# A diffusion trunk on one core: moving modulation tiles out of the front units, and handing every second low half to GpSimd

## The reference, cut to what matters

```python
sh1, sc1, g1, sh2, sc2, g2 = split(silu(c) @ w_mod + b_mod)     # modulation, one set for each group of tokens
h  = rmsnorm(x, norm1_g) * (1 + sc1) + sh1
u, q, k, v, z, xbc, dt = split(h @ w_in)                        # pooling, attention, state-space scan
gates = sigmoid(h @ w_gate + b_gate)
merged = sum(gate_i * (branch_i @ w_branch_i))                  # three branches
x  = x + g1 * (merged @ w_out)
h2 = rmsnorm(x, norm2_g) * (1 + sc2) + sh2
a, b = split(dwconv3(h2 @ w_up))
x  = x + g2 * ((silu(a) * b) @ w_down)
```

## Time and profile before

| what | us |
|---|---|
| three runs | 1495.09, 1491.16, 1492.04 (median 1492.04) |
| span of the profiled execution, first to last instruction | 1489.1 |
| PE busy | 1371.9 |
| DVE busy | 1080.2 |
| ACT busy | 650.6 |
| POOL busy | 221.1 |
| mean granted TensorE clock | 0.965 of full speed |

### The profile page before, as it was taken

One profiled execution on the slowest core, in us unless ns is written; L12 is line 12 of the kernel. 1 busy time (PEld: TensorE's weight loads), 2 busy tenths in 40 slices (PEclk: granted clock), 3 DMA queues, 4 the chain that ended last, 5 costly groups with the idle time before them and its releaser, 6 DMA issues.

```text
span 1489.1 us, 20142 instructions
## 1 busy us (share of the span) xinstructions
PE 1371.9 (92%) x7704; PEld 1320.6 (89%) x7704; DVE 1080.2 (73%) x1827; ACT 650.6 (44%) x1025; POOL 221.1 (15%) x202
## 2 busy tenths in 40 slices
...
GB/s 366 112 145 222 230 110 87 111 87 85 99 114 113 133 148 145 156 133 246 244 128 113 205 220 155 87 112 85 85 94 106 140 95 160 156 155 126 128 129 43
DMA packets 58143, 208.93 MB, mean 140 GB/s; under 512 B 6720, under 2 KB 8768, under 8 KB 56640
## 3 DMA queue, kind: packets, MB, share of 16 engines
...
...
HBM read 203.95 MB, written 3.68 MB: 139 GB/s over the span
## 4 chain that ended last, share of the span: by engine, by line
PE 73%; DVE 15%; ACT 6%; issue 4%; POOL 1%; DMA 1%; SPq 0%; ACTq 0%; DVEq 0%
PE acc L718 21%; PE acc L720 21%; PE acc L719 21%; DVE junk_front L1373 6%; DVE wl L1322 3%; PE mix L948 2%; PE mix L926 2%; PE mix L705 1%; ACT cv L1059 1%; PE mix L853 1%; DVE gates L1482 1%; ACT wh L1025 1%; POOL wl L598 1%; PE mix L881 1%; DMA head<-in_whead_dram 1%
## 5 line engine op out<-in xcount | busy, mean ns | idle before, releaser
L718 PE MATMUL acc<-hh,wh 128*128 128x386 f32 x1600 | 569.7, 356 | 56.0 <-POOL wl L598 25.3
L720 PE MATMUL acc<-hh,wl 128*128 128x386 f32 x1600 | 555.0, 347 | 0.0
L719 PE MATMUL acc<-hl,wh 128*128 128x386 f32 x1600 | 554.5, 347 | 0.0
L1322 DVE TENSOR_TENSOR wl<-raw,wh 128x1024 fp32r<-128x1024 f32 (+1 forms) x264 | 325.8, 1235 | 164.9 <-ACT wh L1025 162.6
L718 PEld LDWEIGHTS acc<-hh,wh 128*128 128x128 f32 x1600 | 311.5, 195 | 70.7 <-POOL wl L598 29.8
L1025 ACT ACTIVATE wh<-raw 128x1024 fp32r<-128x1024 f32 (+1 forms) x280 | 291.2, 1041 | 166.7 <-PE acc L720 166.7
L719 PEld LDWEIGHTS acc<-hl,wh 128*128 128x128 f32 x1600 | 313.2, 196 | 2.9 <-issue 0.6
L720 PEld LDWEIGHTS acc<-hh,wl 128*128 128x128 f32 x1600 | 311.4, 195 | 0.0
L1373 DVE SCALAR_TENSOR_TENSOR junk_front<-rawm,crow 128x1024 f32<-128x1024 f32 x96 | 155.3, 1654 | 0.0
L718 PE MATMUL acc<-ah,wh 128*128 128x386 f32 x352 | 119.4, 339 | 0.0
L719 PE MATMUL acc<-al,wh 128*128 128x386 f32 x352 | 119.3, 339 | 0.0
...
## 6 DMA issues: line engine op xcount, KB each, us to landing
...
```

The costliest lines, as they stand in the source:

```text
L718: mm(out, sh, mhi, start=start, stop=False)
L719: mm(out, sh, mlo, start=False, stop=False)
L720: return mm(out, sl, mhi, start=False, stop=stop)
L1322: tt(wl[:, s, 0:n], raw[:, raw_slot(u), 0:n], wh[:, s, 0:n].bitcast(F32), ALU.subtract).then_inc(lo_done, 1)
```

## The change

Three things change.

1. `mod_after` becomes a table, `MOD_PLACES`. In layer 0 the front carries 16 tiles behind units 8 to 23 and none behind 0 to 7; 8 tiles stand behind units 62 to 69 (the last branches and OUT), 14 behind every third UP unit and 22 behind DOWN units 116 to 137. So layer 0 also makes the first 28 tiles of layer 1, which then has 12 behind units 12 to 23 and 8 in UP. For units 62 to 69 there is a further copy of the silu rows, `crow_late`: a load on POOL at unit 58, and two tanh and two silu instructions at unit 61.
2. `POOL_LO` grows from 8 to 63 units a layer: 3 to 14, then the odd ones from 27 to 65 and from 75 to 135.
3. POOL's program becomes one loop over the units, in which the low half of unit u+3 comes first and the other work has its place by unit (pooling at 12, 14, 17, 20; merges two at a time at 57 to 60).

```diff
-POOL_LO = range(AHEAD, AHEAD + 8)
+POOL_LO = frozenset([*range(AHEAD, AHEAD + 12), *range(MIX0 + 3, OUT0 + 3, 2), *range(UP0 + 3, NU - 4, 2)])
+FRONT = range(UU0, MIX0)
+LATE_ROWS = BRANCH0 + 9
+LATE = range(LATE_ROWS + 1, LATE_ROWS + 9)
+LATE_DONE = OUT0 + 6
...
+def mod_places():
+    tiles = [(l, m) for l in range(DEPTH) for m in range(MODT)][MOD_HEAD:]
+    units = [(0, u) for u in FRONT] + [(0, u) for u in LATE]
+    units += [(0, UP0 + 3 * i + 2) for i in range(14)] + [(0, DOWN0 + i) for i in range(22)]
+    units += [(1, MIX0 - 12 + i) for i in range(12)] + [(1, UP0 + 5 * i + 4) for i in range(MODT - MOD_G2)]
+    return dict(zip(units, tiles, strict=True))
...
 def mod_after(l, u):
-    if u < MOD_G2 - MOD_HEAD:
-        return (l, MOD_HEAD + u)
-    if UP0 <= u < DOWN0 and (u - UP0) % G2_EVERY == G2_EVERY - 1 and (u - UP0) // G2_EVERY < MODT - MOD_G2:
-        return (l, MOD_G2 + (u - UP0) // G2_EVERY)
-    m = u - DOWN0 - 2
-    return (l + 1, m) if 0 <= m < MOD_HEAD and l + 1 < DEPTH else None
+    return MOD_PLACES.get((l, u))
...
+POOLING = (UU0 + 4, UU0 + 6, UU0 + 9, UU0 + 12)
...
+                for u in range(NU):
+                    if u == UP0:
+                        group_done(pool, l, G_OF[(OUT, KT - 1)])
+                        pool.dma_start(crow[:, :, :], cvec_rows).then_inc(crow_in, 16)
+                    if u + AHEAD in POOL_LO:
+                        lo(l, u + AHEAD)
+                    if u == 4:
+                        clear_pads(l)
+                    if u in POOLING:
+                        pooling(l, POOLING.index(u))
...
+                    if BRANCH0 + 5 <= u < BRANCH0 + 9:
+                        for j in (2 * (u - BRANCH0 - 5), 2 * (u - BRANCH0 - 5) + 1):
+                            pool.wait_ge(gb_done, count(l, 24, KT + j))
+                            nc.gpsimd.tensor_tensor(gates[:, j, :], gates[:, j, :], gates[:, KT + j, :], ALU.add) \
+                                .then_inc(mg_done, 1)
+                    if (l, u) == (0, LATE_ROWS - 3):
+                        pool.wait_ge(h_lo, count(l, NSPLIT, SP_Z + 3))
+                        pool.dma_start(crow_late[:, :, :], cvec_rows).then_inc(crow_in, 16)
+                    if OUT0 <= u < UP0:
+                        sum_square(u - OUT0, KT * (2 * l + 1))
...
+                    if (l, u) == (0, LATE_ROWS):
+                        row_tanh(1, crow_late, junk_late)
...
-                junk = junk_front if u < UP0 else junk_ffn
+                junk, rows = (junk_front, crow) if u < MIX0 else (junk_late, crow_late) if u < UP0 else (junk_ffn, crow)
...
+                    if (l, u) == (0, LATE_ROWS):
+                        rows_silu(1, crow_late, junk_late)
                     modulation(l, u)
-                    if u == MOD_G2 - MOD_HEAD - 1:
-                        summed(l, MOD_HEAD, MOD_G2)
+                    if u == MIX0 - 1:
+                        summed(l, MOD_HEAD, MOD_HEAD + KT)
+                        step.then(ts(g1h[:, :, :], mod[:, 2 * KT:3 * KT, :], 0.5, None, ALU.mult))
+                    if u == LATE_DONE:
+                        summed(l, MOD_HEAD + KT, MOD_G2)
                         scale_of(sc2, prm_("n2g", 0, KT), 4 * KT).then_inc(scale_ready, 1)
```

More of the change, by code:

```diff
@@ L84 @@
 DOWN0 = U_OF[(DOWN, 0, 0)]
-G2_EVERY = 5
-G2_LAST = UP0 + G2_EVERY * (MODT - MOD_G2) - 1
-HEAD_LAST = DOWN0 + MOD_HEAD + 1
-PREP = HEAD_LAST + 1
-POOL_LO = range(AHEAD, AHEAD + 8)
-MIX0 = U_OF[(ZZ, 0, 0)]
+PREP = DOWN0 + MOD_HEAD + 2
+MIX0 = U_OF[(ZZ, 0, 0)]
+UU0, BRANCH0, OUT0 = U_OF[(UU, 0, 0)], U_OF[(BRANCH, 0, 0)], U_OF[(OUT, 0, 0)]
+POOL_LO = frozenset([*range(AHEAD, AHEAD + 12), *range(MIX0 + 3, OUT0 + 3, 2), *range(UP0 + 3, NU - 4, 2)])
+LO_NUMBER = {}
+_n = [0, 0]
+for _u in range(DEPTH * NU):
+    _n[_u % NU in POOL_LO] += 1
+    LO_NUMBER[_u] = _u % NU in POOL_LO, _n[_u % NU in POOL_LO]
+FRONT = range(UU0, MIX0)
+LATE_ROWS = BRANCH0 + 9
+LATE = range(LATE_ROWS + 1, LATE_ROWS + 9)
+LATE_DONE = OUT0 + 6
 def closing_unit(g):
@@ L99, in lo_number @@
 def lo_number(n):
-    on_pool = n % NU in POOL_LO
-    return on_pool, sum((i % NU in POOL_LO) == on_pool for i in range(n + 1))
+    return LO_NUMBER[n]
 def done_after(u):
@@ L287, in build @@
             junk_front = sb("junk_front", [P, 2, D], where=a)
+        with ExitStack() as a:
+            sb("under_late", [P, 24 * T + 8 * T], where=a)
+            crow_late = sb("crow_late", [P, 2, D], where=a)
+            junk_late = sb("junk_late", [P, 2, D], where=a)
         with ExitStack() as a:
@@ L663, in _ @@
[L663 to L677 removed]
+                pool.wait_ge(pads, l + 1)
@@ new lines, in pooling @@
+                pool.wait_ge(u_in, count(l, 4, j))
+                step.then(nc.gpsimd.tensor_tensor(tmp[0][:, 1:UW], ut[:, j, 0:UW - 1], ut[:, j, 1:UW], ALU.add))
+                lo, cur = 1, 0
+                for i in range(j):
+                    s = 1 << i
+                    lo += s
+                    hi = UW - (lo - 1)
+                    step.then(nc.gpsimd.tensor_tensor(tmp[1 - cur][:, lo:hi], tmp[cur][:, lo - s:hi - s],
+                                                      tmp[cur][:, lo + s:hi + s], ALU.add))
+                    cur = 1 - cur
```

158 lines of the change are left out of this document (72 added, 86 removed).

## The result

The change takes **1531.8 us** (median of 4 runs, 1531.1 to 1534.7) against 1492.8 for the kernel before (1491.2 to 1495.1): ratio 1.0266, 95% interval 1.0251 to 1.0280. It is slower by 39 us. The profiled execution has a span of 1532.9; it was the slowest of its four, and that of the kernel before the fastest of its own, so differences of the two profiles come out some 5 us larger than the 39.0 of the medians. Beside the other runs the kernel before took 1492.6 to 1493.9 (median of each set), and their ratios are against that.

A forecast was written before the change was run, and what follows sets the result against it. PE was taken as the bound in UP and DOWN, DVE with POOL's blocks in the fronts. Terms -44.2 + 12.8 + 12.6 + 2.7 + 37.5 + 9.1 = +30.5 on 1492.0 gave 1522.5 us; eight-in-ten range 1464 to 1542.

The forecast's parts named there:

- main case: Whole kernel: low halves on POOL block DVE and the change is slower, 1500 to 1542 us, chance 0.68.
- central step: Wherever DVE has no time to spare: each low half moved to POOL costs DVE 2.13 us and saves 1.13.
- fronts, units 4 to 23, both layers: Without tiles beside the early units, PE runs at its own pace: gains of 25.6 and 24.0 us.
- late hand-over to the attention: Later pooling brings DVE to the attention about 5.1 us late, 2.3 to spare: 2.7 us given back per layer.
- attention slots: In the attention, POOL's low half falls on ACT's exponentials and costs nothing.
- scan: POOL's low half holds DVE, costing 1.6 us in each of four steps, two layers: +12.8 (0 to 19).
- branches and OUT, layer 0: Low halves on POOL, late silu rows and tiles load a full DVE: +12.6 us (7 to 16).
- UP and DOWN, layer 0: Tiles and blocks make DVE the bound, last update at 798.4 against 760.2: +37.5 us (0 to 48).
- UP, layer 1: Blocks and eight tiles make DVE late, PE ending at 1389.6 against 1380.46: +9.1 us (0 to 14).
- blocks that nobody feels: Rival, chance 0.20: DVE's waits absorb the blocks; UP, scan and most of DOWN cost nothing: -31, 1461 us.
- Blocks only beside tiles: Rival, chance 0.07: UP's products escape, DOWN pays blocks and six more tiles, scan half: -5, 1487 us.
- the fronts do not run free: Rival, chance 0.05: POOL's one queue or ACT holds front units near 6.9 us, removing the gain: about 1560 us.

The follow-up runs named there:

- front_only: The change, but POOL makes low halves only for units 3 to 14, all others back on DVE: 1463.3 us.
- nmb_cols: The whole change, but the attention's two-column nmb multiplication is two instructions of one column each: 1523.4 us.
- ffn_only: The change, but POOL makes low halves only for units 3 to 14 and every second one of UP and DOWN: 1502.3 us.
- after_dve: The change without any low half on POOL, pooling at units 9 to 12 instead of 12 to 20: 1460.6 us.

## Why the prediction was right, and where it was off

The direction, the mechanism and the range held: 1531.8 for a predicted 1522.5, in the range of 1500 to 1542 of the main case. Its central step, that a low half on POOL blocks DVE for longer than the 1.13 it saves, is what the runs show: the 102 low halves that POOL makes behind the front cost 68.5 us, and without them the change is faster than the kernel before. The size of 2.1 us is right for the tiles and the scan's `ee` (2.1 to 2.2 lost); of the 44 `th<-th,cv` in UP, 31 were caught and lost 1.3 (1.87 for 0.56), as the prediction had it (1.8 to 2 us). One reading behind it was wrong: the taps at 82.47 do not stand beside a low half, which had ended at 79.00 + 2.34 = 81.34, so that row shows nothing of an exemption. The exemption is real all the same; the trace after has the rows (last section).

Term by term, on the profiled executions:

| term | predicted | measured |
|---|---|---|
| fronts, units 4 to 23, both layers | -49.6 | -47.7 |
| late hand-over to the attention | +5.4 | +9.4 (units 24 to 27) |
| attention slots | 0 | +5.7 |
| scan | +12.8 | +6.7 |
| branches and OUT, layer 0 | +12.6 | +17.0 |
| branches and OUT, layer 1 | +2.7 | +6.0 |
| UP and DOWN, layer 0 | +37.5 | +36.5 |
| UP, layer 1 | +9.1 | +6.9 |
| start | 0 | +3.4 |
| sum | +30.5 | +44.0 (spans: +43.8) |

That the total came near is luck in part. The hand-over, the slots and the branches were 17.4 us too cheap, the scan and UP of layer 1 were 8.3 too dear, and these are steps of their own whose errors happened to offset each other.

- *Fronts.* Right: units 4 to 19 take 4.26 each. What is missing stands in the V units (4.48 and 5.14 for units 21 and 22).
- *"I give back 2.7 in each layer."* The lateness was right, its cause half right, and the term too small. Counted from the first matmul of unit 24, DVE begins the attention of layer 0 after 12.0 us where it took 7.1, 4.8 late for my 5.1, and PE takes up its result (L867, now L897) 2.4 late for my 2.7. But the later pooling alone does not do it: in front_only, which has it, DVE comes 2.6 late, PE takes the result up only 0.4 late, and the Z units take 31.1 as before. The other 2.2 are the last tile, blocked by the low half of unit 27. And the term came to 4.8 and 4.6 instead of 2.7, because `nmb` is blocked as well: without that it is 2.0 and 1.9 (nmb_cols).
- *"In the attention slots POOL's low half falls on ACT's exponentials: nothing."* This is the step that failed. I looked for DVE instructions with two SBUF inputs; there the one that is caught, `nmb`, has one, and it took 1.32 to 2.07 us instead of 0.17. It cost 5.7 us in the slots for my 0, part of it gone in nmb_cols (slots 52.5 and 52.7 for 54.6 and 55.2). The passage of the Trainium skill that the prediction draws on (SBUF — State Buffer, "Who interferes with whom") frees an instruction with one SBUF input only "outside the 2-port perf modes"; the prediction left this condition out.
- *Scan.* The block came as worked out: one `ee` in each of four steps per layer, 2.49 instead of 0.35, and PE waits 1.43 for it:

```profile
339.23 2.45 POOL L605 TENSOR_TENSOR wl<-raw,wh 128x1024 fp32r<-128x1024 f32 x1 [12.04 <-ACT wh L1055]
339.33 3.28 DVE L1597 SCALAR_TENSOR_TENSOR ee<-ee,dtt,bg 128x128 f32<-128x128 f32 x4
...
343.27 0.65 PE L978 MATMUL mix<-ee,xt 128*64 128x128 f32 x4 [1.43 <-DVE eb L1601]
```

  Units 47, 49 and 51 paid 1.50 each for my 1.6, unit 45 only 0.65, and unit 43 became 1.84 shorter (8.85 to 7.01), a term that I had at nothing: the net is half of mine. What the traces show there is a gain from the hand-over. Before, DVE stood 4.50 us in its order before a low half whose `wh` was not made yet, and the state work for which PE waits (`xw`) came behind it. Timeline before, DVE and PE, and then after, where the low half is POOL's and PE does not wait:

```profile
313.70 1.23 DVE L1322 TENSOR_TENSOR wl<-raw,wh 128x1024 fp32r<-128x1024 f32 x1 [4.50 <-ACT wh L1025]
...
316.17 0.68 DVE L1529 TENSOR_TENSOR xw<-xt,wdc 128x512 f32<-128x512 f32 x1
...
316.91 0.48 PE L910 MATMUL mix<-xw,bg 128*128 128x256 f32 x1 [1.58 <-DVE xw L1529]
```
```profile
298.80 0.68 DVE L1561 TENSOR_TENSOR xw<-xt,wdc 128x512 f32<-128x512 f32 x1
```

  From the first matmul of unit 43 (310.73 before, 297.08 after) `xw` starts after 5.44 us and 1.72.
- *Branches and OUT.* The low halves on POOL cost 4.0 us in layer 0 (77.9 against 73.9) and 6.2 in layer 1 (67.1 against 60.9), for my 3.1 and 2.7. Rows and tiles cost 13.0 for my 9.5: the rows 6.6 for 4.4, the tiles 6.4 for 5.1. The lag of 2.7 at the last update, still standing, measured as 3.5 (units 66 to 71).
- *UP.* My pairs were 7.8 us long with 2.4 and 3.2 for tiles, so six units with two tiles 3 x 7.8 + 5.6 = 29.0; units 96 to 101 took 29.17 (599.21 to 628.38). UP alone came to +22.3 and DOWN to +14.3; in front_only they are +1.3 and +3.7 by the tiles alone, so some 5 us of the 36.5 are tiles and 32 are low halves. The sign I gave was 27 for UP: it came to 5 less and DOWN to 4 more than I had, so this sum too is nearer than its parts. In layer 1 it was 6.9 for 9.1.
- *Start.* The clock, not the change. Windows after, and of ffn_only, which has the same start:

```profile
52.00:60.00 8.00, 8.00 (x40) 8.00 (x39) 3.09 (x7) 0.00 (x0) 0.00 (x0) 0.50 0.00 1
```
```profile
52.00:60.00 8.00, 5.63 (x37) 5.54 (x37) 4.42 (x12) 1.56 (x4) 0.00 (x0) 0.65 0.00 1
```

  In the change PE ran all of this stretch at a granted clock of 0.50, its lower level of 1.2 GHz; in ffn_only at 0.65 on average. Unit 1 takes 20.5 us in the one and 17.8 in the other; it took 20.4 in front_only and after_dve and 17.8 in the kernel before. So it belongs to the single execution: the other three runs of ffn_only took 3.8 to 5.0 us longer than its profiled one (1502.0 to 1503.2 against 1498.2).

The rival "blocks that nobody feels" decided at a block of under 0.45 us per low half in UP; the mean rise of `th<-th,cv` alone is 0.91. "Blocks only beside tiles" falls by the same rows, and "the fronts do not run free" by the 4.26 us of units 4 to 19.
